# Gate products of the first group on two 64-row halves of the array, and shorter inverse square roots

## What is computed

```python
r = jax.nn.sigmoid(jnp.einsum('blnc,ncd->blnd', xb, wa).reshape(B, L, D_A) + ba)
i = jax.nn.sigmoid(jnp.einsum('blnc,ncd->blnd', xb, wx).reshape(B, L, D_A) + bx)
log_a = -C_RGLRU * jax.nn.softplus(-lam.astype(jnp.float32)) * r.astype(jnp.float32)
a = jnp.exp(log_a)
u = jnp.sqrt(jnp.maximum(-jnp.expm1(2.0 * log_a), 0.0)) * (i * x).astype(jnp.float32)
```

## Time and profile before

| | |
|---|---|
| median of 3 runs | 996.0 us (995.4 to 997.31) |
| the profiled execution's own time | 996.84 us |
| its span, first to last instruction | 995.1 us |
| mean granted PE clock | 0.975 of full |
| busy: PE, DVE, ACT, POOL | 926.3, 676.6, 515.5, 149.5 us |
| the gate products (L514), busy | 32.8 us in 128 passes |

### The profile page before, as it was taken

How to read it: one execution, slowest core, us unless ns; L and a number is a source line. 1 busy time by engine, 2 the same in 40 slices (tenths; PEclk the granted TensorE clock), 3 DMA queues, 4 the chain that set the end, 5 groups by cost and what they waited for, 6 DMA issues and landing times. The chain is left out here.

```text
span 995.1 us, 20265 instructions
## 1 busy us (share of the span) xinstructions
PE 926.3 (93%) x7822; PEld 668.3 (67%) x7822; DVE 676.6 (68%) x1901; ACT 515.5 (52%) x1050; POOL 149.5 (15%) x208
## 2 busy tenths in 40 slices
PE   5698967999999999999999999999999999999987
PEld 3455856568665867587757775786668675867554
DVE  3455788847784787568774878577847875687445
ACT  2634679443853476337733584438533863366321
POOL 4000010201130113011201112001301130111112
PEclk9797997999999999999999999999999999999998
DMA  9995202100110011001010011001101010100413
GB/s 312 323 310 169 85 2 86 64 1 23 43 64 2 23 43 65 1 22 43 26 41 23 1 44 65 2 23 43 65 1 44 1 51 1 44 1 29 117 43 114
DMA packets 46619, 61.15 MB, mean 61 GB/s; under 512 B 2748, under 2 KB 40208, under 8 KB 46524
## 3 DMA queue, kind: packets, MB, share of 16 engines
q1 hardware_dynamic: 46524, 59.86, 18.4%
HBM read 48.90 MB, written 10.95 MB: 60 GB/s over the span
## 5 line engine op out<-in xcount | busy, mean ns | idle before, releaser
L404 PE MATMUL ring<-hnh,wih 128*128 128x256 bf16 (+1 forms) x1152 | 290.9, 264 | 3.1 <-DVE wil L1348 3.1
L404 PE MATMUL ring<-hnh,wil 128*128 128x256 bf16 (+1 forms) x1152 | 290.7, 263 | 0.6 <-issue 0.6
L404 PE MATMUL ring<-hnl,wih 128*128 128x256 f16 (+1 forms) x1152 | 290.7, 263 | 0.0
L404 PE MATMUL ring<-woh,work 128*128 128x512 f16 x512 | 162.1, 379 | 0.0
L404 PEld LDWEIGHTS ring<-hnh,wih 128*128 128x128 f16 x1152 | 110.7, 98 | 14.7 <-issue 3.1
L404 PEld LDWEIGHTS ring<-hnh,wil 128*128 128x128 bf16 x1152 | 110.5, 98 | 13.1 <-issue 0.7
L404 PEld LDWEIGHTS ring<-hnl,wih 128*128 128x128 f16 x1152 | 110.5, 98 | 12.8
L873 ACT ACTIVATE qh<-qq 128x256 bf16<-128x256 f32 x96 | 41.5, 432 | 142.7 <-PE lev L404 83.0
L404 PE MATMUL ring<-wih,hnh 128*128 128x512 f16 (+1 forms) x264 | 100.1, 379 | 0.0
L404 PE MATMUL ring<-wih,hnl 128*128 128x512 f16 (+1 forms) x264 | 100.1, 379 | 0.0
L404 PE MATMUL ring<-wil,hnh 128*128 128x512 bf16 (+1 forms) x264 | 100.1, 379 | 0.0
(11 more groups left out here) (327 smaller groups left out, 1887.5 us busy)
## 6 DMA issues: line engine op xcount, KB each, us to landing
xin<-in_x_prompt_dram SPq DMA_DIRECT2D x16, 512.0 KB, 3.8
work<-in_x_prompt_dram SPq DMA_DIRECT2D x16, 512.0 KB, 4.6
out_dram<-work SPq DMA_DIRECT2D x16, 512.0 KB, 2.6
work<-in_ada_w_dram SPq DMA_DIRECT2D x5, 1024.0 KB, 11.3
wol<-in_w_in_dram SPq DMA_DIRECT2D x5, 1024.0 KB, 9.0
woh<-in_ada_w_dram SPq DMA_DIRECT2D x4, 1024.0 KB, 13.2
woh<-in_w_in_dram SPq DMA_DIRECT2D x4, 1024.0 KB, 10.8
work<-in_w_out_dram SPq DMA_DIRECT2D x4, 1024.0 KB, 5.5
```

The lines of the kernel that those rows point to most:

```text
L404: last = mm(out, a(k), b(k), start=start and k == ks[0] and j == 0, stop=stop and k == ks[-1] and j == 2)
```

## The change

- Gate products: `wg` now holds, for each 128-channel tile, both gates of a block side by side: rows 0 to 63 have the r block in columns 0 to 63 and the i block in 64 to 127, rows 64 to 127 the other way round. Each product contracts 64 rows, and the two halves of the array write two banks (`aux[0]` and `aux[1]`). A call is again four float32 products of 256 columns. The memset of `wg` goes, since no zeros are left.
- `gates` now makes one signal, `g_ps`, and waits for `kt_sb` before its first product.
- `gates_out`: r of a tile lies on 64 partitions of each bank, so each sigmoid covers 64 partitions: 8 activations a call where there were 4. For i, source and target partitions differ (64 to 127 read, 0 to 63 written, and the reverse), with a bias row `bxs` whose halves are swapped; two small transfers load it.
- `rsqrt_steps`: 9 operations where there were 12 (one for the start value, a second-degree step, one Newton step).
- The decode part is changed in the same way.

```diff
-NEWTON = 12
+NEWTON = 9
...
+RC0, RC1, RC2 = 1.87661677, -1.25213721, 0.375520627
...
-        wg = sb("wg", [P, 2, CT, P])
+        wg = sb("wg", [P, CT, P])
...
+            rows = rg_bx[0].rearrange("(r c) -> r c", c=P)
+            for half in range(2):
+                sp.dma_start(am[ROW["bxs"]:ROW["bxs"] + CT, 0, 64 * half:64 * half + 64],
+                             rows[:, 64 - 64 * half:128 - 64 * half]).then_inc(par_ld, 16)
...
-                            sp.dma_start(wg[64 * odd:64 * odd + 64, w, :, 64 * odd:64 * odd + 64], v).then_inc(wg_ld, 16)
+                            o = 64 * (odd ^ w)
+                            sp.dma_start(wg[64 * odd:64 * odd + 64, :, o:o + 64], v).then_inc(wg_ld, 16)
...
             def gates(n, p):
                 pe.wait_ge(cvc.sem, cvc.at(n, 8 * p + 8))
-                for w, s in ((0, gr_ps), (1, gi_ps)):
-                    if p == 0 and w == 0:
-                        if not isinstance(n, int) or n > 0:
-                            pe.wait_ge(ytl.sem, ytl.at(n - 1, 2))
-                    elif w == 1:
-                        pe.wait_ge(kt_sb.sem, kt_sb.at(n, p + 1))
-                    elif not (isinstance(n, int) and n == BODIES - 1):
-                        pe.wait_ge(hn_lo.sem, hn_lo.at(n + 1, 2))
-                    for c in range(2):
-                        last = mm(aux[(1 + w + p) % 2][:, T * c:T * c + T], wg[:, w, 2 * p + c, :], xc[:, c, :],
-                                  start=True, stop=True)
-                    last.then_inc(s.sem, 1)
+
+                if p == 0:
+                    if not isinstance(n, int) or n > 0:
+                        pe.wait_ge(ytl.sem, ytl.at(n - 1, 2))
+                elif not (isinstance(n, int) and n == BODIES - 1):
+                    pe.wait_ge(hn_lo.sem, hn_lo.at(n + 1, 2))
+                pe.wait_ge(kt_sb.sem, kt_sb.at(n, p + 1))
+                for c in range(2):
+                    for odd in range(2):
+                        rows = slice(64 * odd, 64 * odd + 64)
+                        last = mm(aux[odd][:, T * c:T * c + T], wg[rows, 2 * p + c, :], xc[rows, c, :], start=True, stop=True)
+                last.then_inc(g_ps.sem, 1)
...
             def gates_out(n, p):
 
-                act.wait_ge(gr_ps.sem, gr_ps.at(n, p + 1))
+                act.wait_ge(g_ps.sem, g_ps.at(n, p + 1))
                 act.wait_ge(iu.sem, iu.at(n, p))
                 for c in range(2):
-                    A(rr[:, c, :], aux[(1 + p) % 2][:, T * c:T * c + T], ACT.Sigmoid,
-                      bias=pcol("ba", 2 * p + c)).then_inc(r_sig.sem, 1)
-                act.wait_ge(gi_ps.sem, gi_ps.at(n, p + 1))
+                    for odd in range(2):
+                        rows = slice(64 * odd, 64 * odd + 64)
+                        A(rr[rows, c, :], aux[odd][rows, T * c:T * c + T], ACT.Sigmoid,
+                          bias=pcol("ba", 2 * p + c)[rows, :]).then_inc(r_sig.sem, 1)
                 act.wait_ge(scan.sem, scan.at(n, 2 * p))
                 for c in range(2):
-                    A(ii[:, c, :], aux[p][:, T * c:T * c + T], ACT.Sigmoid, bias=pcol("bx", 2 * p + c)).then_inc(i_sig.sem, 1)
+                    for odd in range(2):
+                        rows, src = slice(64 * odd, 64 * odd + 64), slice(64 - 64 * odd, 128 - 64 * odd)
+                        A(ii[rows, c, :], aux[odd][src, T * c:T * c + T], ACT.Sigmoid,
+                          bias=pcol("bxs", 2 * p + c)[src, :]).then_inc(i_sig.sem, 1)
...
                 done(V.tensor_scalar(v, ssq, 1.0 / count, EPS, ALU.mult, ALU.add))
-                done(V.tensor_scalar(t.bitcast(I32), v.bitcast(I32), 1, None, ALU.logical_shift_right))
-                done(V.tensor_scalar(y.bitcast(I32), t.bitcast(I32), -1.0, MAGIC, ALU.mult, ALU.add))
-                for _ in range(3):
-                    done(V.tensor_tensor(t, y, y, ALU.mult))
-                    done(V.scalar_tensor_tensor(t, t, -0.5, v, ALU.mult, ALU.mult))
-                    done(V.scalar_tensor_tensor(y, t, 1.5, y, ALU.add, ALU.mult))
+                done(V.tensor_scalar(y.bitcast(I32), v.bitcast(I32), -0.5, MAGIC, ALU.mult, ALU.add))
+                done(V.tensor_tensor(t, y, y, ALU.mult))
+                done(V.tensor_tensor(t, t, v, ALU.mult))
+                done(V.scalar_tensor_tensor(t, t, RC1 / RC2, t, ALU.add, ALU.mult))
+                done(V.scalar_tensor_tensor(y, t, RC0 / RC2, y, ALU.add, ALU.mult))
+
+                done(V.tensor_tensor(t, y, y, ALU.mult))
+                done(V.scalar_tensor_tensor(t, t, -0.5 * RC2 ** 3, v, ALU.mult, ALU.mult))
+                done(V.scalar_tensor_tensor(y, t, 1.5 * RC2, y, ALU.add, ALU.mult))
```

More of the change, by code:

```diff
@@ L68 @@
 _at = 0
-for _name, _n in (("pre", KT), ("post", KT), ("cw", CW * CT), ("cb", CT), ("ba", CT), ("bx", CT), ("lam", CT),
+for _name, _n in (("pre", KT), ("post", KT), ("cw", CW * CT), ("cb", CT), ("ba", CT), ("bx", CT), ("bxs", CT), ("lam", CT),
                   ("lbl", CT), ("onw", CT), ("adab", 3 * KT)):
@@ L176, in build @@
         u_ps = Signal("u_ps", 4)
-        gr_ps, gi_ps = Signal("gr_ps", 2), Signal("gi_ps", 2)
+        g_ps = Signal("g_ps", 2)
         f_sig, k_sig, q_sb = Signal("f_sig", 2), Signal("k_sig", 2), Signal("q_sb", 2)
@@ L183, in build @@
         xa_sb, ga_sil = Signal("xa_sb", 2), Signal("ga_sil", 2)
-        r_sig, i_sig, a_exp, th_ok = (Signal(s, 4) for s in ("r_sig", "i_sig", "a_exp", "th_ok"))
+        r_sig, i_sig = Signal("r_sig", 8), Signal("i_sig", 8)
+        a_exp, th_ok = Signal("a_exp", 4), Signal("th_ok", 4)
         u_sqrt = Signal("u_sqrt", 2)
@@ L449, in turn_y @@
                     pe.wait_ge(yb_ok.sem, yb_ok.at(n, 8))
[L450 to L452 removed]
+                    pe.wait_ge(i_sig.sem, i_sig.at(n, 8))
                 for h in range(2):
@@ L564, in body @@
                 else:
-                    pe.wait_ge(i_sig.sem, i_sig.at(n - 1, 4))
+                    pe.wait_ge(i_sig.sem, i_sig.at(n - 1, 8))
                 project(ring[0], FR, 0, n)
@@ L719, in _ @@
                 if b == 0:
-                    pe.wait_ge(par_ld, 160)
+                    pe.wait_ge(par_ld, 192)
                     nc.tensor.transpose(aux[0][:, 0:NROW], am[0:NROW, 0, :], ident[0:NROW, 0:NROW]).then_inc(pre_ps, 1)
@@ L728, in _ @@
             pe.wait_ge(wg_ld, 64)
-            pe.wait_ge(zeroed, 3)
+            pe.wait_ge(zeroed, 2)
             pe.wait_ge(carry_zero, 2)
@@ L797, in _ @@
             pe.wait_ge(dv("conv_d"), 16)
[L798 to L801, removed]
+            for c in range(CT):
+                for odd, bank in ((0, lev[1]), (1, aux[0])):
+                    rows = slice(64 * odd, 64 * odd + 64)
+                    last = mm(bank[:, TD * c:TD * c + TD], wg[rows, c, :], xcd[rows, TD * c:TD * c + TD], start=True, stop=True)
             last.then_inc(dv("gates_ps"), 1)
@@ L931, in gates_out @@
             def gates_out(n, p):
-                act.wait_ge(gr_ps.sem, gr_ps.at(n, p + 1))
+                act.wait_ge(g_ps.sem, g_ps.at(n, p + 1))
                 act.wait_ge(iu.sem, iu.at(n, p))
                 for c in range(2):
-                    A(rr[:, c, :], aux[(1 + p) % 2][:, T * c:T * c + T], ACT.Sigmoid,
-                      bias=pcol("ba", 2 * p + c)).then_inc(r_sig.sem, 1)
-                act.wait_ge(gi_ps.sem, gi_ps.at(n, p + 1))
+                    for odd in range(2):
+                        rows = slice(64 * odd, 64 * odd + 64)
+                        A(rr[rows, c, :], aux[odd][rows, T * c:T * c + T], ACT.Sigmoid,
+                          bias=pcol("ba", 2 * p + c)[rows, :]).then_inc(r_sig.sem, 1)
                 act.wait_ge(scan.sem, scan.at(n, 2 * p))
                 for c in range(2):
-                    A(ii[:, c, :], aux[p][:, T * c:T * c + T], ACT.Sigmoid, bias=pcol("bx", 2 * p + c)).then_inc(i_sig.sem, 1)
+                    for odd in range(2):
+                        rows, src = slice(64 * odd, 64 * odd + 64), slice(64 - 64 * odd, 128 - 64 * odd)
+                        A(ii[rows, c, :], aux[odd][src, T * c:T * c + T], ACT.Sigmoid,
+                          bias=pcol("bxs", 2 * p + c)[src, :]).then_inc(i_sig.sem, 1)
             def decay(n, p):
-                act.wait_ge(r_sig.sem, r_sig.at(n, 2 * p + 2))
+                act.wait_ge(r_sig.sem, r_sig.at(n, 4 * p + 4))
                 for c in range(2):
@@ L1131, in _ @@
             act.wait_ge(dv("gates_ps"), 1)
-            for w, dst, bias in ((0, rrd, "ba"), (1, iid, "bx")):
+            for dst, bias, w in ((rrd, "ba", 0), (iid, "bxs", 1)):
                 for c in range(CT):
-                    o = W4 * w + TD * c
-                    A(dst[:, TD * c:TD * c + TD], lev[1][:, o:o + TD], ACT.Sigmoid, bias=pcol(bias, c)).then_inc(dv("ri_d"), 1)
-            act.wait_ge(dv("ri_d"), 2 * CT)
+                    for odd, bank in ((0, lev[1]), (1, aux[0])):
+                        rows, src = slice(64 * odd, 64 * odd + 64), slice(64 * (odd ^ w), 64 * (odd ^ w) + 64)
```

(10 more changed lines are left out.)

5 lines of the change are left out of this document (1 added, 4 removed).

## The result

| | before | after |
|---|---|---|
| median | 996.49 us (995.4 to 997.31, 4 runs) | 1024.27 us (1023.07 to 1024.84, 4 runs) |
| ratio, 95% interval | | 1.0278 [1.026, 1.0296] |
| span of the profiled execution | 995.1 us | 1023.1 us |
| mean granted PE clock | 0.975 | 0.962 |

A forecast was written before the change was run, and what follows sets the result against it. PE, 93% busy, was taken to be held by ACT and DVE chains at its waits mid-body and nearly so at body end; 6.6 + 5.5 - 2.0 = +10.1 us gave 1006 us, range 1000 to 1015.

The forecast's parts named there:

- Sigmoids: ACT in gates_out: a half sigmoid takes 0.36 us like a whole one, so four more add 1.43 us per call.
- neighbours on different partitions don't overlap: Rival at ACT's sigmoids: 0.47 us each, 13.5 us on top, 1020; chance 0.11 shared with the slow-clock case.
- Middle of the body: At level(n, 1, 5): sigmoids +1.43, root -0.60, so +0.83 us per body; eight bodies +6.6; PE waits 2.5 us.
- End of the body: After gates_out(n, 1): later ACT work delays the next body, +0.79 us each; seven ends +5.5; new wait before turn_y.
- Gate products: PE's gate calls: both halves run together, -0.7 us at p = 0, -0.6 at p = 1, hidden under PE's waits.
- The 0.1 more at p = 1: Gate call at p = 1: estimated 0.1 us extra because the next product's float32 weights can't be loaded early.
- Inverse roots: DVE's root: three fewer operations of 0.20 us save 0.60 us on each chain with a root.
- The rest: After the last body and in decode: gates and roots save, together -2.0 us; setup transfers and missing memset 0.
- wait for `kt_sb`: Before the first gate product: ACT's copy is covered by PE's output projection, 0 us; uncovered up to 0.59.
- The clock: Rival: each long PE wait brings 3.4 us at 1.2 GHz, 7 x 1.7, 1018; chance 0.11 shared with slower sigmoids.

The follow-up runs named there:

- after_filled: Changed kernel plus 14 extra products on PE (1.5 us) just ahead of the wait before level(n, 1, 5); 1023.75 us, ratio 1.0277.
- before_halves: Kernel before, old products and root, with only the gates' sigmoids split into halves of 64 partitions, none crossing halves; 1034.7 us, ratio 1.0391.
- gates_only: Changed kernel with the old twelve-operation root put back; 1033.74 us, ratio 1.0386.
- half_products: Kernel before with the second tile's gate products left out, 4 passes per call instead of 8, sigmoids and root unchanged; 991.62 us, ratio 0.9954.
- rsqrt_swap: Kernel before with the nine-operation root, and ACT doing heads(n, 1, 4) before the sigmoids of gates_out(n, 0); 1009.34 us, ratio 1.0128.

## Why the prediction was right or wrong

*Sigmoids*: **this is the step that failed.** It took 0.36 us for a half, because "partitions don't count", from copies of 32 and 128 partitions. They showed the duration, and there it held (468 and 470 ns). But the cost in a row of sigmoids is the distance between starts, and 0.36 was that of neighbours on the same partitions. With alternating halves it is 0.494: +2.52 us per call instead of +1.43. I had this as a rival, "neighbours on different partitions don't overlap", at 1020. It held, at a slightly higher price than the 0.47 that I gave it, and I had weighed it too low. I had said that nothing in the trace spoke for it; nothing spoke against it either, and the nearest row was about another quantity.

The Trainium skill, in "ScalarE: Activation LUTs", section "What ACT_TABLE_LOAD costs", says that ACTIVATEs back to back overlap by about 93 ns. The runs agree where the partitions stay (0.463 long, 0.373 apart) and disagree where they change (0.469 long, 0.494 apart). I had not looked for the condition.

*Middle of the body*: right, with that term mis-sized. By the same working, 2.52 - 0.60 = +1.92 us a body. The bodies of `after_filled` without a drop of the clock took 26.01 between their gates, 24.10 before: +1.91. The drop adds 1.25 by the same run, and 24.10 + 1.92 + 1.25 = 27.27 stands against the 27.24 of the changed kernel. The wait is 3.43 us, forecast at 2.5 and 3.6 with the true spacing.

*End of the body*: the chain of reasons held; its working with 2.52 gives +1.88 us, and the bodies without a drop show 82.88 - 81.30 = +1.58, so it was 0.3 too much. The wait came at the projection, for `i_sig`, and not at `turn_y`: I had left that wait of PE's list out.

*Gate products*: right in size (1.80 to 1.07 us, forecast -0.7) and in being hidden beside the slower sigmoids, by `before_halves` against `gates_only`. The Trainium skill's factor of up to two from contractions of at most 64 ("TensorEngine Tiling (Array Packing)", section "Overview") did appear inside the call, 1.7 with the switches counted in, and the time did not follow. The switches cost about 0.1 us each, as I had taken them. The 0.1 more at p = 1, for float32 weights, did not show: both calls hold PE for 1.07 us, and the saving there is 0.66 only because that call had been shorter before, 1.73. `half_products` refines one point: in the kernel before, two fifths of such a saving would have counted (5.1 of 13 us).

*Inverse roots*: right, 0.60 per chain. *The rest*: from the last body's gates to the end, +0.1 was measured; +0.8 for its middle less 2.0 was forecast, and the 1.1 us more that the sigmoids take account for all but 0.2 of the difference. The one 5.1 us wait for `kt_sb`, at gates(0, 1), which I had put at 0, cost no more than the rest of that body gave back: from body 0's gates to body 1's `gates_only`, which has this wait, took 116.4 us, and `before_halves`, which waits 3.6 us for `hnl` there, 116.3.

*The clock*: named as a rival, with the right place and the drop of 3.4 us, and small as I had said: about 3 us, 2 of them from `after_filled` and 1.1 from the longer stretch in body 1.

*Together*: the sum of the prediction with 2.52 is 1006 + 15 x 1.09 = 1022.4, and 3 for the clock makes 1025.4, against 1024.27. The sum is closer than its parts, which is in part luck: the end-of-body term is 7 x 0.3 = 2 us too high, and the +1.0 us ahead of body 0, which I hadn't, makes up for half of that. In the ten other kernels' profiles body 0's gates started between 128.6 and 131.4 us, so that +1.0 lies within what moves anyway. Body 1 took 4.9 where others took 3.8, because it had 6.8 us at 1.2 GHz instead of 3.4, as its middle of 28.60 us shows; why it had them was not tried and stays open.

## What to carry to other kernels

When a change makes the matrix products cheaper by spreading results over partition halves, price the engine that reads them first: here each call saved 0.7 us of PE and cost 2.52 us of ACT, on the one chain that PE was already waiting for. Price an instruction in a row by the distance between starts of neighbours that are like the new ones in every operand, not by its duration, and if no row has such neighbours, give the end where they don't overlap a real chance. If work must be cut into halves, keep neighbours on the same partitions (some 10 us here), or cut by columns.

## What the runs showed of the hardware

- In these runs (sigmoids of float32 from the banks, with a bias column) ACT overlaps a sigmoid with the one before only while both the partitions read and the partitions written stay the same: 0.373 us from start to start for 64 by 256, against 0.48 when either changes, and 0.494 when every step changes. Where something changes, the next one starts some 25 ns after the end of the one before (0.457 and 0.469 us long).
- The duration does not depend on the number of partitions (468 ns for 64, 470 for 128). On all partitions, halving the columns from 256 to 128 brought the distance from 0.36 to 0.25 us.
- Two 64-row products on the two halves of the array start 7 ns apart, and the pairs 0.216 us apart: two float32 passes of 256 columns in the time of one. The step into the halves and the step out of them took about 0.1 us more each (0.32 and 0.31 us).
- In bodies 2 to 6 of the changed kernel 3.43 us without a product were followed, some 1.3 us after PE had started again, by 3.4 us at 1.2 GHz. In body 1 the low clock began within the same wait and lasted 6.8 us. With 14 products in the gap the clock stayed at 2.4 GHz in two of these six bodies. The same wait need not bring the same clock: of the seven waits of 2.80 us in `rsqrt_swap`, three had a drop.
